# A Mamba-2 mixer rewritten: decays from four row quarters with masks added in PSUM, projections in another order, constants loaded ahead of x

## The reference, cut to what matters

```python
def adaln(c, w, b):
    mod = jax.nn.silu(c) @ w + b
    shift, scale, gate = jnp.split(mod[:, None, :], 3, axis=-1)
def mamba2_mixer(h, w_in, conv_w, conv_b, dt_bias, a_log, d_skip, norm_w, w_out):
    z, xbc, dt = split_cols(h @ w_in, SSM_SPLITS)        # 2048, 3072, 32 columns
    xbc = silu(causal_conv(xbc, conv_w, taps=4) + conv_b)
    xs_, Bm, Cm = split_cols(xbc, (D_INNER, G * N, G * N))
    dt = jax.nn.softplus(dt + dt_bias)
    a = dt * -exp(a_log)
    # over all 256 tokens at once, for each of 32 heads, l >= s:
    # y[l] = sum_s (C[l].B[s]) * exp(cum[l] - cum[s]) * x[s] * dt[s]
    y = y + d_skip[:, None] * x
    y = y.reshape(B, T, D_INNER) * jax.nn.silu(z)
    y = rmsnorm(y.reshape(B, T, G, D_INNER // G), norm_w)   # G = 4
    return y @ w_out
```

## Time and profile before

| | us |
|---|---|
| median of 3 runs | 3271.74 (3271.71 to 3272.78) |
| the profiled execution, its time | 3273.18 |
| its span, first to last instruction | 3271.4 |
| TensorE busy | 2985.1 (91%) |
| VectorE busy | 1511.8 (46%) |
| ScalarE busy | 693.6 (21%) |
| hybrid mixer, to its residual | 0 to 234.9 |
| dense block, to its residual | 234.9 to 471.4 |
| Mamba-2 mixer: projections and what follows them | 482.7 to 674.5 |
| its loop over heads | 674.5 to 726.9 |
| z, norms | 726.9 to 754.1 |
| its down projection | 754.1 to 817.9 |
| all that follows | 817.9 to 3271.4 |

### The profile page before, as it was taken

One profiled execution on the slowest core, in us unless ns is written; L12 is line 12 of the kernel. 1 busy time (PEld: TensorE's weight loads), 2 busy tenths in 40 slices (PEclk: granted clock), 3 DMA queues, 4 the chain that ended last, 5 costly groups with the idle time before them and its releaser, 6 DMA issues.

```text
span 3271.4 us, 51615 instructions
## 1 busy us (share of the span) xinstructions
PE 2985.1 (91%) x22970; PEld 2067.5 (63%) x22970; DVE 1511.8 (46%) x2941; ACT 693.6 (21%) x1061; POOL 90.1 (3%) x76
## 2 busy tenths in 40 slices
PE   5888999979799999999999797698999999988898
PEld 4777988868433333333333344388999985678898
DVE  5656777956201101101101248418888844364454
ACT  1323330130100000000000211314433421311343
POOL 1000000030000000000000000000000000032000
PEclk8898999988899999999999898689999999999999
DMA  6755655605799899999899222015566622010452
GB/s 265 271 180 200 274 235 228 231 4 193 292 369 374 351 359 368 354 360 372 340 361 373 76 77 77 1 39 193 206 221 230 244 104 90 1 67 2 149 185 79
DMA packets 96950, 686.82 MB, mean 210 GB/s; under 512 B 10576, under 2 KB 13776, under 8 KB 13904
## 3 DMA queue, kind: packets, MB, share of 16 engines
q1 hardware_dynamic: 94064, 678.47, 54.2%
q10 hardware_dynamic: 2656, 4.97, 0.4%
HBM read 682.35 MB, written 1.05 MB: 209 GB/s over the span
## 4 chain that ended last, share of the span: by engine, by line
PE 76%; DVE 15%; ACT 5%; issue 2%; DMA 2%; POOL 0%; DVEq 0%; SPq 0%; ACTq 0%; POOLq 0%
PE ps L476 34%; PE ps L1795 18%; PE ps L792 7%; PE ps L1818 6%; PE ps L712 5%; DVE macc L558 4%; PE ps L1821 3%; DVE AR L2180 2%; DVE FR L773 2%; DMA ring<-W 1%; ACT FR L757 1%; PE ps L1803 1%; DMA cst<-CS 1%; PE ps L687 1%; DVE macc L555 1%
## 5 line engine op out<-in xcount | busy, mean ns | idle before, releaser
L1795 PE MATMUL ps<-AR 128*32 128x512 f32 x4080 | 535.2, 594 | 7.5 <-ACT HT L1878 7.5
L476 PE MATMUL ps<-HT,ring 128*128 128x256 f32 (+1 forms) x1600 | 451.2, 444 | 26.9 <-ACT HT L650 20.5
L1906 DVE TENSOR_TENSOR AR<-AR,ps 128x256 f32<-128x256 f32 x84 | 35.6, 423 | 811.6 <-ACT AR L1870 811.6
L476 PEld LDWEIGHTS ps<-HT,ring 128*128 128x128 f32 x1600 | 311.3, 196 | 156.8 <-issue 114.6
L476 PE MATMUL ps<-FR,FR 128*128 128x256 f32 x3120 | 396.5, 288 | 7.8 <-DVE FR L773 6.1
L476 PEld LDWEIGHTS ps<-FR,FR 128*128 128x128 f32 x3120 | 386.3, 195 | 8.9 <-issue 3.6
L558 DVE SCALAR_TENSOR_TENSOR macc<-ring,SC,macc 128x256 f32<-128x256 f32 x960 | 390.9, 483 | 0.0
L792 PE MATMUL ps<-FR,FR 128*128 128x256 f32 x2832 | 349.2, 283 | 0.0
L1795 PEld LDWEIGHTS ps<-AR 128*32 128x32 f32 x4080 | 150.5, 110 | 307.1 <-issue 294.4
L792 PEld LDWEIGHTS ps<-FR,FR 128*128 128x128 f32 x2832 | 343.9, 192 | 0.0
L773 DVE TENSOR_TENSOR FR<-ring,FR 128x2048 fp32r<-128x2048 f32 x129 | 294.2, 2291 | 98.7 <-ACT FR L757 98.5
(11 more groups left out here) (393 smaller groups left out, 2565.7 us busy)
## 6 DMA issues: line engine op xcount, KB each, us to landing
ring<-W SPq DMA_DIRECT2D x441, 1024.0 KB, 5.8
AR<-W SPq DMA_DIRECT2D x205, 1024.0 KB, 8.0
XT<-XIN ACTq DMA_DIRECT2D x2, 1024.0 KB, 14.1
cst<-CS ACTq DMA_DIRECT2D x1, 1787.0 KB, 25.7
out<-XT SPq DMA_DIRECT2D x1, 1024.0 KB, 4.5
sml<-SM ACTq DMA_DIRECT2D x1, 890.5 KB, 24.4
cst<-CS ACTq DMA_DIRECT2D x1, 128.5 KB, 22.9
C<-SM ACTq DMA_DIRECT2D x1, 4.0 KB, 5.2
```

Source lines behind the costliest of these rows:

```text
L476: ins = g.matmul(out, l, r, **kw)
L1795: ins = g.matmul(bank.ap[group(i), :], mo.hg[e % 2][:, 4 * h + k, group(t)], w[n][:, k, :], start=j == 0 and k == 0, stop=j == 1 and k == ...
L1906: g.tensor_tensor(mo.hu[b % 2], mo.sg[b % 2], counts.bank(p + ".gu", b)[:, 256:512], MUL).then_inc(*s.done(p + ".hu", b, empties=(p + ".gu ...
```

## The change

In words: the constants are issued ahead of `x`, and the scaling of the first norm goes over VectorE and ScalarE as in the other stages (`norm_dve`, `shift_act`), POOL having no part in it; the wait for `sml`, which stood behind six steps of VectorE, now stands ahead of the first. The background steps stand elsewhere: more of them in the hybrid stage, so that those of ada0 begin in the dense stage, 14 instead of 17 in the projections, and in the down projection TensorE's come after the slots as (0, 0, 0, 1, 1, 1, 2, 3), while VectorE does its 8 as before. In the mixer dt comes first, then B and C, x, and z last. ScalarE does one tap of the convolution; softplus, sums, B times C and transposes stand between projections. The decays of 4 heads are 4 matmuls with 32 rows each, at another row quarter of TensorE each, on a copy `ma.cum` of the cumulated sums; a matrix `future` with -1e30 above the diagonal is added by 8 matmuls into the same banks, and ScalarE takes the exp out of PSUM with the subtraction as its bias. VectorE multiplies with `ma.cb`, adds D x, and multiplies by z, pair by pair; squares, sums and roots stand in the loop, and the down projection begins after the first of four groups of the norm.

```diff
+def ssm_steps(n):
+    return 0 if n == 0 or n <= 12 and n % 2 == 0 else 1
 (schedule, hybrid part)
     for u in range(9):
         load("hyb_in")
-        bg.go()
+        bg.go(2 if u in (6, 7) else 1)
...
     for i in range(4):
         load("hyb_out")
-        bg.go()
+        bg.go(2 if i < 2 else 1)
...
-    for n in range(20):
+    for n in range(21):
         load("ssm_in")
-        bg.go(1 if n < 8 or n % 4 else 0)
-    load("ssm_in")
+        bg.go(ssm_steps(n))
 (hybrid_pe)
             g.wait_ge(s_in["cst"], 16)
-            for _ in range(5):
+            for _ in range(8):
                 bg.go()
             norm_pe(g, s, "hy")
             bg.finish("hyb_mod")
...
             for u in (HY_K, HY_Q):
                 rows(u)
-                bg.go()
+                bg.go(2)
...
-                    later={4: [("hy.oB", 1)]})
+                    later={2: [("hy.oB", 1)]}, steps=(2, 2, 1, 2))
 (hybrid_dve)
-            for _ in range(6):
-                bg.go()
-            s.wait_ge("norm.root", "hy", 0)
-            g.reciprocal(RN[:, 0:256], RN[:, 0:256]).then_inc(*s.done("norm.rstd", "hy", 0))
             g.wait_ge(s_in["sml"], 16)
             bg.finish("hyb_mod")
             s.own()
...
+            norm_dve(g, s, "hy", HT, mod_weight("hyb_mod", 0))
...
-            for _ in range(4):
-                bg.go()
+            bg.go(6)
             ps = pair2(counts.bank("hy.in", HY_K))
...
-            for i in range(4):
-                bg.go()
+            bg.go(7)
             residual_dve(g, s, "hy.down", ("down", "hy.down", 3), MN["hyb_gate"][0], 0)
 (mamba_pe)
+            def decays(i):
+
+                b = [counts.take("ma.dec", 4 * i + q) for q in range(4)]
+                for q in range(4):
+                    s.wait_emptied(b[q])
+                for q in range(4):
+                    h, r = 4 * i + q, slice(32 * q, 32 * q + 32)
+                    g.matmul(b[q].ap[:, 0:384], bc(cs("ident", 32 * q + h, 32 * q + h + 1, (32 * q, 32 * q + 32)), (32, 128)), ma.cum[r, :],
+                             start=True, stop=False, skip_group_check=True)
+                for q in range(4):
+                    for c in (0, 256):
+                        ins = g.matmul(b[q].ap[:, c:c + 128], ident, cs("future"), start=False, stop=True, skip_group_check=True)
+                    ins.then_inc(*s.done("ma.dec", 4 * i + q))
...
-            s.wait_ge("ma.cb", 3, 2)
-            for h in range(36):
-                if h < 32:
-                    ah = [bc(ma.av[:, x, h:h + 1], (128, 128)) for x in range(2)]
-                    b = counts.take("ma.dec", h)
-                    s.wait_emptied(b)
-                    mm(g, b.ap[:, 0:128], [(ah[0], cs("tri"))])
-                    mm(g, b.ap[:, 128:256], [(ah[0], ones), (ah[1], cs("tri"))]).then_inc(*s.done("ma.dec", h))
...
+            s.wait_ge("ma.cum")
+            for i in range(9):
+                if i < 8:
+                    decays(i)
+                if i:
+                    outputs(i - 1)
+                if i >= 3 and i % 2:
+                    sums((i - 3) // 2)
+            spread_pe(g, s, "ma.rms0", 7, 2)
+            acc = down_begin("ma.down")
+            for i in range(8):
+                if i == 1:
+                    sums(3)
+                if i in (1, 2):
+                    spread_pe(g, s, f"ma.rms{i}", 7 + 2 * i, 2)
+                if i == 2:
+                    spread_pe(g, s, "ma.rms3", 13, 2)
+                down_slot(g, s, "ma.down", "ssm_out", i, 8, acc, lambda k: ma.y[:, k, :], [("ma.g", 2 * i + 1)])
+                bg.go((0, 0, 0, 1, 1, 1, 2, 3)[i])
 (mamba_act)
+            for h in range(32):
+                e, ps = ma.E[h % 8], counts.bank("ma.dec", h)
+                s.wait_ge("ma.dec", h).wait_ge("ma.nc")
+                if h >= 8:
+                    s.wait_ge("ma.y_ps", (h - 8) // 2)
+                g.activation(e[:, 0:256], ps[:, 0:256], ACT.Exp, bias=ma.nc[:, 0, h:h + 1]).then_inc(*s.done("ma.ex0", h))
+                g.activation(e[:, 256:384], ps[:, 256:384], ACT.Exp, bias=ma.nc[:, 1, h:h + 1]).then_inc(*s.done("ma.ex", h, empties=("ma.dec", h)))
+                if h >= 9 and h % 2:
+                    square((h - 9) // 2)
+                if h in (17, 25):
+                    q = h // 8 - 2
+                    root_act(g, s, f"ma.rms{q}", 7 + 2 * q, 2, 512)
 (mamba_dve)
+            for h in range(32):
+                e = ma.E[h % 8]
+                s.wait_ge("ma.ex", h)
+                g.tensor_tensor(e, e, ma.cb[:, h // 8, :], MUL).then_inc(*s.done("ma.w", h))
+                if h >= 5 and h % 2:
+                    output((h - 5) // 2)
...
             for i in range(8):
                 bg.go()
             residual_dve(g, s, "ma.down", ("down", "ma.down", 7), MN["ssm_mod"][0], 16)
 (scalar)
             g.dma_start(C1[:, :], SM[:, 0:8]).then_inc(s_in["c"], 16)
+            g.dma_start(cst[:, 0:EARLY], CS[:, 0:EARLY]).then_inc(s_in["cst"], 16)
             g.dma_start(XT[:, :, 0:256], XIN[0].rearrange("(k p) t -> p k t", p=128)).then_inc(s_in["x"], 16)
-            g.dma_start(cst[:, 0:EARLY], CS[:, 0:EARLY]).then_inc(s_in["cst"], 16)
```

More of the change, by code:

```diff
@@ new lines, in down_begin, with down_slot @@
+        def down_begin(x):
+            return [counts.take(x, m, keep=True) for m in range(4)]
+        def down_slot(g, s, x, name, i, n, acc, rhs, ready, load=True, free=True):
+            sl = slot(name, i)
+            w = flat(sl).rearrange("p (k c) -> p k c", k=2)
+            if load:
+                wait_slot(s, sl)
+            for one_ready in ready:
+                s.wait_ge(*one_ready)
+            for kk in range(2):
+                k = 2 * i + kk
+                for m in range(8):
+                    h = m % 2
+                    if k == 0:
+                        s.wait_emptied(acc[m // 2])
+                    ins = g.matmul(acc[m // 2].ap[:, h * 256:h * 256 + 256], w[:, kk, m * 128:m * 128 + 128], rhs(k),
+                                   start=k == 0 and h == 0, stop=k == 2 * n - 1 and h == 1, skip_group_check=True)
+            ins.then_inc(*s.done("down", x, i, frees=(sl,) if free else ()))
@@ new lines, in outputs @@
+            def outputs(i):
+                for k in (2 * i, 2 * i + 1):
+                    y = counts.take("ma.y", k)
+                    s.wait_emptied(y).wait_ge("ma.w", 2 * k + 1)
+                    for x in range(2):
+                        for o in range(2):
+                            h = 2 * k + o
+                            ins = g.matmul(y.ap[64 * o:64 * o + 64, 128 * x:256], ma.xdt[:, x, h, :], ma.E[h % 8][:, 256 * x:256 + 128 * x],
+                                           start=x == 0, stop=x == 1, skip_group_check=True)
+                    ins.then_inc(*s.done("ma.y_ps", k))
@@ new lines, in sums @@
+            def sums(q):
+                sums_pe(g, s, f"ma.rms{q}", [[(t, ma.sq[:, 4 * (q % 2) + k, t * 128:t * 128 + 128]) for t in range(2)] for k in range(4)],
+                        lambda k: s.wait_ge("ma.sq", 4 * q + k))
+            norm_pe(g, s, "ssm")
+            bg.finish("ssm_mod")
+            s.wait_marks("dn.end")
+            norm_done(s, "ssm")
+            i = slot("ssm_in", 0)
+            b = counts.take("ma.dtS")
+            s.wait_emptied(b)
+            wait_slot(s, i)
@@ new lines, in mamba_pe @@
+            thin(g, b.ap[:, 0:256], by8(i), lambda k: HT[:, k, 0:256]).then_inc(*s.done("ma.dtS_ps", frees=(i,)))
+            project(1)
+            b = counts.take("ma.dt")
+            s.wait_emptied(b).wait_ge("ma.dtS")
+            for x in range(2):
+                ins = mm(g, b.ap[:, 32 * x:32 * x + 32], [(ma.dS[:, x * 128:x * 128 + 128], cs("sel"))])
+            ins.then_inc(*s.done("ma.dt_ps"))
+            for n in (2, 3, 4):
+                project(n)
+            b = counts.take("ma.cum")
@@ L1525, in mamba_pe @@
+            down_end("ma.down")
             s.mark("ma.end")
@@ L1554, in mamba_act, with square @@
+            for n in range(13, 21):
+                ps = counts.bank("ma.in", n)
+                s.wait_ge("ma.in", n)
+                j = n - 13
+                g.activation(ma.z[:, 2 * j:2 * j + 2, :], pair2(ps), ACT.Silu).then_inc(*s.done("ma.pr", n, empties=("ma.in", n)))
+                if n < 15:
+                    silu(n - 2)
+            def square(k):
+                q = k // 4
+                s.wait_ge("ma.yz", k)
                 if q >= 2:
                     s.wait_ge(f"ma.rms{q - 2}.sums")
-                j = 4 * (q % 2)
@@ L1561, in mamba_act @@
+            for k in range(12, 16):
+                square(k)
+            for q in (2, 3):
+                root_act(g, s, f"ma.rms{q}", 7 + 2 * q, 2, 512)
             s.mark("ma.end")
@@ L1619, in mamba_dve, with gated @@
+            def gated(q):
                 rstd_dve(g, s, f"ma.rms{q}", 7 + 2 * q, 2)
```

289 lines of the change are left out of this document (126 added, 163 removed).

## The result

The changed kernel takes 3302.42 us in the median of 4 runs (3298.86 to 3304.68) beside 3272.26 for the kernel before (4 runs, 3271.71 to 3276.41): ratio 1.0088, 95% interval 1.0071 to 1.0106, so 30 us slower. The forecast was 3313, slower. The profiled execution is the fastest of the four (span 3297.0).

What follows compares the result with a forecast made beforehand. TensorE was taken to bound the kernel, holding 76% of the chain of waits, VectorE 15%. The terms summed to +41.6, so 3314.8 us as a profiled execution and 3313 as a median, range 3285 to 3337.

Steps and rivals of the forecast that it cites:

- The down projection: Mixer's down projection: TensorE and VectorE wait in turn through the ring, residual at 129 us for 63.8, +65.2.
- the chain: Mixer's down projection: from out4 on, slot, sum, product and landing follow each other with no overlap, within the +65.2.
- The loop: Loop over heads, z and norms: 50 us for 79.6, four heads in 4.3 us for 6.6, -29.6.
- Rival B: Loop's quarter matmuls don't overlap, +15; a lower clock adds up to 10: 3328 to 3338, chance 0.13.
- Start: Up to the first projection: VectorE's wait for sml stands ahead of its first product, +1.5.
- Hybrid stage: Background steps added in the hybrid stage: +0.6 in its middle and +5.2 in its down projection.
- the middle: Hybrid stage before its down projection: two extra background steps ahead of a tile TensorE waits for, +0.6.
- Dense block: Dense blocks: waits on VectorE partly vanish, -4; longer ada0 products at the end, +7.7.
- Projections: Mixer's projections to the loop: 187 us for 191.8, with 18 of waiting and slow restarts, -5.
- Rival C: Down projection: the ring holds no chain, so it keeps 63.8 plus three norm groups; kernel 3251, chance 0.08.
- D: Down projection's chain shorter, with warm slots, quick landings and a start gaining from early constants: 3285 to 3300, chance 0.17.
- A: The forecast itself: the chain of the down projection sets its length, 3302 to 3326, chance 0.62.

Runs made afterwards that it cites:

- early_sums: The changed kernel with TensorE's background steps in the mixer's down projection after the slots as (1, 0, 1, 1, 1, 1, 1, 2): 3255.87 us.
- before_late_sums: The kernel before with TensorE's background steps in the mixer's down projection as (0, 0, 1, 1, 1, 1, 2, 2) instead of one each: 3343.72 us.
- masks_twice: The changed kernel with each of the eight mask matmuls of a group of four heads made twice: 3311.13 us.
- one_quarter: The changed kernel with all four decay matmuls of a group on row quarter 0: 3327.03 us.
- sml_wait_late: The changed kernel with VectorE's eight products of hyb_mod ahead of its wait for sml: 3288.90 us.
- cst_behind_x: The changed kernel with the constants issued behind x again, as before the change: 3300.69 us.

## Why the prediction was right, point by point

**The down projection (+65.2, measured +61.3).** The mechanism and the size were right. early_sums takes the chain away and with it 43 of the 61 us; the other 18 are the norm between the slots and VectorE's finish and b0 at the end, which the working had in its sum as well. The stage took 125.1 for 129: a18 ended 27.0 us after the first slot began, for 29.9, and the three turns took 20.8 each for the 21.2 worked out. What was wrong is the count of the kernel before, the step that its slot 0 sums and the order of its slots; it didn't enter the sum, but it made the expectation of before_late_sums miss by 54 us.

**The loop (-29.6, measured -27.8).** Four quarters were taken at 0.75 by the 64-row row and took 0.93; a group of four heads takes 4.29 (684.05 to 688.34), forecast 4.3. That the matmuls pay for changing modes is as the trace of before had it, about 0.2: eight masks take 1.98 to the start of the next matmuls, where eight more of the same kind in masks_twice add 1.79. The Trainium skill (TensorEngine Tiling (Array Packing), Key Properties) has the drain at a change of mode, and neither trace shows it to be more. Rival B, quarters that don't overlap, falls: one_quarter shows what that would be. Its second half, the low clock, came true in small: 12 us of the loop ran at 0.71 and 0.72. The eight profiled kernels with the unedited loop take 49.1 to 51.8 for it, forecast 50.

**Start (+1.5, measured -0.7).** `sml` landed at 21.67 instead of the 23 taken, which is the 1.3, and the rest went 0.9 quicker. The step, the wait for `sml` on VectorE, was right, and sml_wait_late prices it: 13.5 us, which the early constants alone couldn't give.

**Hybrid stage (+5.8, measured +9.8).** The term that was mis-sized is the middle, +4.3 for +0.6; the other, +5.5 for +5.2, was right. Over the eight profiled kernels with the change's distribution the stage takes 185.3 to 189.1 from its first projection to its residual, over the four with the old one 177.7 to 178.5: +8.5 in the mean, 3.5 of it in the middle. The changed kernel's TensorE at the tile that waits for VectorE, and the slot behind it:

```profile
117.20 1.16 PE L480 MATMUL ps<-AR 64*128 64x128 f32 x14 [2.46 <-DVE AR L1252]
118.38 8.86 PE L480 MATMUL ps<-ring,HT 128*128 128x256 f32 x32
```

and that slot in the kernel before, where nothing waits ahead of it:

```profile
115.39 7.17 PE L476 MATMUL ps<-ring,HT 128*128 128x256 f32 x32
```

All eight have this wait of 2.46, none of the four has it. So the step named was right, VectorE's two more products ahead of a tile that TensorE needs, but its price left out the slow slot behind the wait (1.7) and took 2.7 back for the finish. At the end of that slot the changed kernel is 5.4 behind (71.2 from the first projection for 65.8); 1.1 comes back up to the down projection.

**Dense block (-4 and +7.7, measured -0.2).** Eight profiled kernels with the change's distribution take 236.3 to 239.7, the four with the old one 236.3 to 236.6: +1.8 in the mean, so the changed kernel's own profile is at the lower end. Of TensorE's three waits for VectorE in the first third the changed kernel keeps the first (3.23 at 281.22, where the earlier trace rows has 3.24); those of 1.66 and 3.71 are gone. That is 5.4 where 4 were taken. One term was put at nothing: the norm at the block's start. As the residual no longer follows TensorE directly, TensorE stands idle for 4.01 instead of 0.69 ahead of the norm's sums, and they take 5.30 for 3.72:

```profile
245.03 5.30 PE L480 MATMUL ps<-HT,cst 128*128 128x256 f32 x16 [4.01 <-ACT HT L636]
```

From the residual to TensorE's first matmuls behind the norm it is 19.6 for 18.1, +1.6 (+2.4 in the mean of the eight). This leaves 3.6 for the longer products at the end (4.8 in the mean), forecast 7.7. The split is worked out, not tried by itself.

**Projections (-5, measured -10.8).** The stretch begins with a norm too, which took 14.0 for 11.4, as its sums took 6.61 for 3.72 at a granted clock of 0.62 (0.80 before); in early_sums, masks_twice and cst_behind_x they took 3.72, so it is no property of the change. The projections proper took 178.3 where 187 were worked out. TensorE waits four times for 2.12 and once for 0.42 on ScalarE's silu, and once for 1.98 on the softplus, 10.9 together; of the slots behind these waits three are slower than 7.07 (7.40, 8.26, 8.76), another 3.2. That is 14 of the 18 us of waiting and restarts; the remaining 5 or so are spread over the other terms and were not taken apart.

**Rivals C and D.** Rival C, no chain in the ring, falls with the first profile. D, a shorter chain, falls too: the slots behind the waits took 8.59 to 9.07, the landing 4.9, and the early constants gave nothing at the start; they do only in sml_wait_late.

**The range.** It held, and 3302.4 lies at the lower edge of A's 3302 to 3326 and 11 below the forecast of 3313. The bounds of A's terms, added up, reach much further than 3302 to 3326 (some 3265 to 3353), so that narrower range was a judgement and not a sum. By stage the errors are between 0.3 and 6.1 us in either direction; the two largest, 6.1 behind the mixer and 5.8 in the projections, make most of the 16 by which the profiled execution (3298.9 for 3314.8) came in lower; that the hybrid stage's 4.0 went the other way and offset a part of them is luck. Most of the 6.1 isn't a property of the change, as said above.

## What to carry to other kernels

When two engines share a ring of buffers through a third party that issues in order, a piece of work that is nearly free (a sum of 0.95 us) can be the release of everything: write down for each slot whose place it takes, what that one waits for, and which slot of the other engine stands ahead of it. If the release stands behind the slot just ahead of the one that it feeds, no two of the steps overlap: three turns of 20.8 us for 7.8 each, some 40 us, and 43 by the experiment. Such a piece must not be moved back for tidiness, and any change in how many background steps earlier stages take shifts the whole count. And a load made earlier gives nothing while the next wait on the engine is for a later one: look at what lands last before the first instruction.

## What the runs showed of the hardware that I had not expected

The granted clock falls to the lower level in the middle of dense work, and a wait ahead of it isn't needed. In the same, unedited loop over the heads two of eight profiles show 6 us at 0.71 right behind a wait of 2.67 on TensorE; the other six show twice some 5 us in which the masks take 3.2 to 3.7 for 2.05, with no wait directly ahead. In early_sums TensorE is busy for 18.4 us without a gap at 1.00, and then come 5.2 us at 0.67; the waits of 1.24 to 1.69 lie behind these stretches, and the clock after them is at 1.00. In one_quarter a wait of 2.67 was followed by 39 us at 0.69, in which TensorE was busy for 36; in masks_twice the whole loop ran at 1.00. So what makes the clock fall isn't shown by these runs, and a profile of one execution can put it in different places: a difference of 2 or 3 us between two such loops shouldn't be given to an edit.
